# First block: output products from three f32r parts, a half of the columns at a time; the modulation computed inside the input projections

## The reference

```python
# first block, layer i
x = layer_norm(ALPHA * x + mixed @ w_out[i], ln_g[i, 0], ln_b[i, 0])
x = layer_norm(ALPHA * x + moe(x, ...), ln_g[i, 1], ln_b[i, 1])
# second block, layer l: the modulation depends on c and on weights only
shift, scale, gate = jnp.split(silu(c) @ ada_w[l] + ada_b[l], 3, axis=-1)
h = rms_norm(x, norm_w[l]) * (1.0 + scale) + shift
...
x = x + gate * (mixed @ w_out[l])
```

## Time and profile before

| | |
|---|---|
| median of 3 runs | 4140.01 us (4139.27 to 4143.25) |
| the profiled execution | 4143.35 us, span of its instructions 4141.7 us |
| mean granted clock of TensorE | 0.899 of 2.4 GHz |
| busy: TensorE / weight loads / VectorE / ACT / GpSimd | 3488.4 / 2668.9 / 1987.1 / 1367.8 / 445.2 us |
| read from HBM, written | 379.68 MB, 73.32 MB |

### The profile page before, as it was taken

How to read it: one execution, slowest core, us unless ns; L and a number is a source line. 1 busy time by engine, 2 the same in 40 slices (tenths; PEclk the granted TensorE clock), 3 DMA queues, 4 the chain that set the end, 5 groups by cost and what they waited for, 6 DMA issues and landing times. The chain is left out here.

```text
span 4141.7 us, 50920 instructions
## 1 busy us (share of the span) xinstructions
PE 3488.4 (84%) x19695; PEld 2668.9 (64%) x19695; DVE 1987.1 (48%) x3438; ACT 1367.8 (33%) x2478; POOL 445.2 (11%) x321
## 2 busy tenths in 40 slices
PE   8999886899829988847959999079988888998878
PEld 6874543788717766634438888068865576885557
DVE  3236455667461436462645756543245434315544
ACT  2026601657430023232025645220144322014442
POOL 0100000334330000000112423300010000001000
PEclk9999998999959899868979999589979998997999
DMA  4243062879540110015246966411100021110011
GB/s 146 89 126 108 1 228 93 299 264 395 196 176 26 50 29 1 1 31 148 102 144 247 346 231 261 182 67 32 31 1 1 31 92 63 32 31 1 1 49 79
DMA packets 247781, 458.80 MB, mean 111 GB/s; under 512 B 44754, under 2 KB 119846, under 8 KB 247206
## 3 DMA queue, kind: packets, MB, share of 16 engines
q1 hardware_dynamic: 229125, 388.64, 27.1%
q0 software_dynamic: 18432, 67.12, 4.2%
HBM read 379.68 MB, written 73.32 MB: 109 GB/s over the span
## 5 line engine op out<-in xcount | busy, mean ns | idle before, releaser
L1602 PE MATMUL psum<-high_in,e_rowsT_high 128*128 128x256 f32 (+1 forms) x1080 | 330.1, 324 | 5.4 <-DVE e_rowsT_low L174 5.4
L1603 PE MATMUL psum<-high_in,e_rowsT_low 128*128 128x256 f32 (+1 forms) x1080 | 326.2, 320 | 0.0
L174 POOL TENSOR_TENSOR low_down<-w_down,high_out 128x1024 fp32r<-128x1024 f32 x64 | 199.4, 3133 | 318.6 <-ACT high_out L1676 318.6
L1602 PEld LDWEIGHTS psum<-high_in,e_rowsT_high 128*128 128x128 f32 x1080 | 206.4, 191 | 22.3 <-issue 6.1
L1603 PEld LDWEIGHTS psum<-high_in,e_rowsT_low 128*128 128x128 f32 x1080 | 206.9, 192 | 16.2
L1183 POOL TENSOR_TENSOR x<-x,ln_bias 128x1024 f32<-128x1024 f32 x16 | 37.9, 2368 | 1313.1 <-DVE x L1157 1313.1
L3248 DVE TENSOR_REDUCE mla_low<-psum 128x1 f32<-128x256 f32 (+7 forms) x128 | 91.0, 752 | 153.2 <-PE psum L3114 153.2
L245 PE MATMUL psum<-ring_high,s_x_high 128*128 128x512 f32 (+3 forms) x768 | 140.1, 326 | 29.0 <-DVE ring_high L169 29.0
L174 DVE TENSOR_TENSOR low_gate<-w_gate,high_in 128x1024 fp32r<-128x1024 f32 x128 | 147.9, 1217 | 0.5 <-issue 0.5
L174 DVE TENSOR_TENSOR low_up<-w_up,high_in 128x1024 fp32r<-128x1024 f32 x128 | 147.9, 1217 | 0.0
L245 PEld LDWEIGHTS psum<-ring_high,s_x_high 128*128 128x128 f32 x768 | 117.2, 196 | 40.9 <-DVE ring_high L169 29.3
(11 more groups left out here) (570 smaller groups left out, 7905.4 us busy)
## 6 DMA issues: line engine op xcount, KB each, us to landing
w_gate<-in_exp_w_gate SPq DMA_DIRECT2D x32, 2048.0 KB, 10.1
w_up<-in_exp_w_up SPq DMA_DIRECT2D x32, 2048.0 KB, 15.1
w_down<-in_exp_w_down SPq DMA_DIRECT2D x32, 2048.0 KB, 21.4
ada<-in_ada_w SPq DMA_DIRECT2D x24, 1024.0 KB, 5.2
expert_rows<-e_out POOLq DMA_DIRECT2D x47, 512.0 KB, 7.0
expert_rows<-zero_row SPq DMA_DIRECT2D x33, 512.0 KB, 7.1
token_rows<-x SPq DMA_DIRECT2D x32, 512.0 KB, 2.6
x<-token_rows SPq DMA_DIRECT2D x24, 512.0 KB, 17.8
```

What stands on the lines that cost most here:

```text
L174: return eng.tensor_tensor(low, whole, high, ALU.subtract)
L1602: pe.matmul(dst, rows_high[:, k, :], w_high[:, k, cols], start=(k == 0), stop=False)
L1603: pe.matmul(dst, rows_low[:, k, :], w_high[:, k, cols], start=False, stop=False)
```

## The change

- **Output products of the first block.** Rows of the mixed features and weights are split into f32r high and low parts, and a product is made of three calls for each feature tile, as in the projections. The 1024 columns are done in halves: all eight row tiles for the first 512 columns, then all eight for the others. Eight banks instead of five. The statistics of a half are taken as soon as it is summed.
- **Early part.** In `memory_attention` SP loads the first half of the weights, and the mixer's 6 (layer 1: 8) feature tiles are split there, one an iteration, the high on ACT and the low on VectorE, each at the end of its iteration. The two memory tiles and the weights are split in `residual_norm`. In layer 1 the high parts of both weight halves share one place: ACT makes the second set after the eighth product (`shared_high`).
- **Order of loads** in `residual_norm`: x tile by tile, each with a semaphore of its own, the second half of the weights, gain and bias.
- **Modulation** moves from `residual_norm` into `project`: layer 0's beside the bias table, layer 1's beside the convolution. VectorE weighs one chunk after each even job from job 2 on, TensorE adds up a chunk after the even job that follows, SP loads two chunks for every chunk of projection weights, and waits for free slots there. ACT's Silu is its first instruction of the stage. The projection has five banks while the modulation is in it. Outputs from job 26 on wait until all chunks are weighed, since they lie where the slots do.
- **The gate row** is stored to DRAM at the end of the projection, and `gated_residual` loads it onto all partitions, behind the 4 MB of x.

Core of the diff:

```diff
+    banks = 5 if modulation else BANKS
     with stage(nc, "weights_loaded0", "weights_loaded1", "products_ready", "even_emptied", "odd_emptied",
-               "x_high", "x_low", "w_high", "w_low", *(beside.SEMAPHORES if beside else ())) as (block, s):
+               "x_high", "x_low", "w_high", "w_low", *(beside.SEMAPHORES if beside else ()),
+               *(modulation.SEMAPHORES if modulation else ())) as (block, s):
...
+                if modulation:
+                    modulation.load(sp, s, c)
                 if beside:
                     beside.store(sp, s, emptied, c)
...
                mm.then_inc(s["products_ready"], 1)
+                if modulation:
+                    modulation.add_up(pe, s, n)
...
+                    if modulation:
+                        modulation.before(eng, s, n)
+                    out(eng, core.bank[n % banks][0:shape[0], 0:shape[1]]).then_inc(emptied[parity], 1)
+                    if modulation and parity == 0:
+                        modulation.weigh(eng, s, n)
...
+            if modulation:
+                modulation.activate(act, s)
...
+        @block.sync
+        def _(sp):
+            for dst, view in weights.loads[0]:
+                sp.dma_start(dst, view).then_inc(s["out_weights"], 16)
+            sp.wait_ge(s["out_weights"], 16 * len(weights.loads[0]))
...
+                if 1 <= i <= len(early.whole):
+                    dve.wait_ge(s["early_high"], i)
+                    leave_low(dve, early.low[i - 1], early.whole[i - 1], early.high[i - 1]).then_inc(s["early_low"], 1)
...
+                if i < len(early.whole):
+                    act.activation(early.high[i], early.whole[i], ACT.Copy).then_inc(s["early_high"], 1)
...
+    mix = Halves(tiles_of(mixT), tiles_of(m.at("mix_low", AT_XT, [P, KT, SEQ], F32R)), tiles_of(m.at("mix_high", AT_WORK, [P, KT, SEQ], F32R)))
+    early = Halves(mix.whole[0:PAIRS], mix.low[0:PAIRS], mix.high[0:PAIRS])
+    loads, raws, lows, highs = [], [], [], []
+    for half in range(2):
+        raw = m.at("w_out", AT_WORK + (32 + 16 * half) * KB, [P, KT, BANK])
+        loads.append([(raw[:, :, :], rows_of(core.io["w_out"][0])[:, :, half * BANK:(half + 1) * BANK])])
+        raws.append(tiles_of(raw))
+        lows.append(tiles_of(m.at("w_out_low", AT_WORK + (32 + 16 * half) * KB, [P, KT, BANK], F32R)))
+        highs.append(tiles_of(m.at("w_out_high", AT_WORK + (64 + 16 * half) * KB, [P, KT, BANK], F32R)))
+    weights = OutWeights(loads, raws, lows, highs, False)
+    memory_attention(nc, core, qm, mixT[:, PAIRS:KT, :], AT_WORK + 96 * KB, weights, early)
+    return mix, weights
...
+    def load(self, sp, s, c):
         io, l = self.core.io, self.l
+        if c == 0:
+            with sp.bass.allow_non_contiguous_dma(reason="a few values a partition"):
+                sp.dma_start(self.c_col[:, :], io["c_2"][0].rearrange("(k p) -> p k", p=P)).then_inc(s["ada_loaded"], 16)
+                sp.dma_start(self.b_col[:, :], io["ada_b_2"][l, 0:2 * D].rearrange("(k p) -> p k", p=P)).then_inc(s["ada_loaded"], 16)
+                sp.dma_start(self.w_col[:, :], io["norm_w_2"][l].rearrange("(k p) -> p k", p=P)).then_inc(s["ada_loaded"], 16)
+            sp.dma_start(self.gate[:, :], broadcast_rows(io["ada_b_2"][l, 2 * D:3 * D])).then_inc(s["ada_loaded"], 16)
+        for j in range(self.SLOTS) if c == 1 else range(2 * c - 1, 2 * c + 1) if c >= 2 else ():
+            if j < self.CHUNKS:
+                if j >= self.SLOTS:
+                    sp.wait_ge(s["ada_ready"], j - self.SLOTS + 1)
+                view = rows_of(io["ada_w_2"][l])[:, :, j * self.WIDTH:(j + 1) * self.WIDTH]
+                sp.dma_start(self.slots[j % self.SLOTS][:, :, :], view).then_inc(s[f"ada_chunk{j % self.SLOTS}"], 16)
+
+    def store(self, sp, s):
+        sp.wait_ge(s["gate_ready"], 1)
+        sp.dma_start(self.core.mod_gates[self.l:self.l + 1, :], self.gate[0:1, :]).then_inc(s["gate_stored"], 16)
+        sp.wait_ge(s["gate_stored"], 16)
...
+    def before(self, eng, s, n):
+        if n >= 2 * self.CHUNKS + self.LAG:
+            eng.wait_ge(s["ada_ready"], self.CHUNKS)
+
+    def weigh(self, dve, s, n):
+
+
+
+        c = n // 2 - self.LAG // 2
+        if c == self.CHUNKS + 1:
+            self.finish(dve, s)
+        if not 0 <= c < self.CHUNKS:
+            return
...
+    def add_up(self, pe, s, n):
+        c = n // 2 - self.LAG // 2 - 1
+        if n % 2 or not 0 <= c < self.CHUNKS:
+            return
...
+    K = len(mix.whole)
+    OWN = K - 2
+    JOBS = 2 * TILES
...
+            for t in range(TILES):
+                sp.dma_start(x[:, t, :], source[t * P:(t + 1) * P, :]).then_inc(s[f"x_loaded{t}"], 16)
+            for dst, view in weights.loads[1]:
                 sp.dma_start(dst, view).then_inc(s["weights_loaded"], 16)
...
+            for n in range(JOBS):
+                half, t = divmod(n, TILES)
+                q = slice(t * P, (t + 1) * P)
+                dst = core.bank[n % BANKS][:, :]
+                high, low = weights.highs[half], weights.lows[half]
+                if n >= BANKS:
+                    pe.wait_ge(s["summed"], n - BANKS + 1)
+                for k in range(K):
+                    if t == 0:
+                        pe.wait_ge(s["w_high"], half * K + k + 1)
+                    if n == 0 and k >= OWN:
+                        pe.wait_ge(s["mem_high"], k - OWN + 1)
+                    pe.matmul(dst, mix.high[k][:, q], high[k], start=(k == 0), stop=False)
+                for k in range(K):
+                    if t == 0:
+                        pe.wait_ge(s["w_low"], half * K + k + 1)
+                    if n == 0 and k >= OWN:
+                        pe.wait_ge(s["mem_low"], k - OWN + 1)
+                    pe.matmul(dst, mix.high[k][:, q], low[k], start=False, stop=False)
+                    mm = pe.matmul(dst, mix.low[k][:, q], high[k], start=False, stop=(k == K - 1))
+            pe.wait_ge(s["summed"], JOBS)
...
+            def lows(half):
+                if half:
+                    dve.wait_ge(s["weights_loaded"], 16 * len(weights.loads[1]))
+                for k in range(K):
+                    if half == 0 and k >= OWN:
+                        dve.wait_ge(s["mem_high"], k - OWN + 1)
+                        leave_low(dve, mix.low[k], mix.whole[k], mix.high[k]).then_inc(s["mem_low"], 1)
+                    dve.wait_ge(s["w_high"], half * K + k + 1)
+                    leave_low(dve, weights.lows[half][k], weights.raws[half][k], weights.highs[half][k]).then_inc(s["w_low"], 1)
+            def add(t, half):
+                cols = slice(half * BANK, (half + 1) * BANK)
+                n = half * TILES + t
+                dve.wait_ge(s["products_ready"], n + 1)
+                if half == 0:
+                    dve.wait_ge(s[f"x_loaded{t}"], 16)
+                summed.settle(dve.scalar_tensor_tensor(out=x[:, t, cols], in0=x[:, t, cols], scalar=ALPHA, in1=core.bank[n % BANKS][:, :],
+                                                       op0=ALU.mult, op1=ALU.add))
+                measured.mark(dve.bn_stats(stats[:, t, half, :], x[:, t, cols]))
+            lows(0)
+            early = TILES if weights.shared_high else 2
+            for t in range(TILES):
+                add(t, 0)
+                if t == early - 1:
+                    lows(1)
+                    add(i, 1)
...
+            for half in range(2):
+                if half:
+                    act.wait_ge(s["weights_loaded"], 16 * len(weights.loads[1]))
+                    if weights.shared_high:
+                        act.wait_ge(s["products_ready"], TILES)
+                for k in range(K):
+                    if half == 0 and k >= OWN:
+                        act.activation(mix.high[k], mix.whole[k], ACT.Copy).then_inc(s["mem_high"], 1)
+                    act.activation(weights.highs[half][k], weights.raws[half][k], ACT.Copy).then_inc(s["w_high"], 1)
...
+    weights = OutWeights(loads, raws, lows, highs, True)
+    memory_attention(nc, core, qm, memT, W + 20 * KB, weights, early)
...
+            sp.dma_start(gate[:, :], broadcast_rows(gate_row)).then_inc(s["gate_loaded"], 16)
...
+            dve.wait_ge(s["gate_loaded"], 16)
```

176 lines of the change are left out of this document (67 added, 109 removed).

## The result

The changed kernel takes **4084.24 us** (median of 4 runs, 4082.28 to 4092.48) beside 4141.63 for the kernel before on the same chip (4139.27 to 4143.82): a ratio of 0.9865, 95% interval 0.9848 to 0.9882. So 57 us are gone where I had forecast 63.

What follows compares the result with a forecast made beforehand. TensorE alone was taken to bound the first block's output products, with weight loads ahead and a tail behind. Terms -36.5 - 44.0 - 8.6 + 14.4 + 3.5 + 5.5 + 2.5 = -63.2 us gave 4077 us, range 4064 to 4102.

Steps and rivals of the forecast that it cites:

- Part 1: Layer 0's output stage to the last sum: f32r calls and early weights take 93.8 us instead of 130.3, -36.5 us.
- Part 2: Layer 1's output stage to the last sum: 120.9 us instead of 164.9, -44.0 us.
- half-turn: Layer 1's products, eighth sum to ninth, where ACT makes the second set of highs: 10.5 us instead of 6.9.
- Part 3: Tails behind the last sum of both output stages: -4.3 us each, -8.6 together, bounds -4 and -12.
- Part 4: Modulation moved into the projections: add-ups +14.4 us for two layers; in layer 1 Silu +3.5, last chunk +5.5.
- last chunk: Layer 1's projection: the modulation's final load stands behind ring load 6, so TensorE waits, +5.5 us (3 to 12).
- Part 5: Memory attention with early highs and lows in each iteration: +2.5 us (0 to 10); gate row read back: nothing.
- (a): Output stage, second half: VectorE's normalisation becomes the bound, 1.5 us more 7 times in layer 0, 4087 us; chance 0.08.
- (b): Layer 1's projection takes its two late transfers at their far ends, 13 and 12 us, 4093 us; chance 0.08.
- (c): Projections: SP's new waits delay some 14 ring loads by three jobs (16.3 us), 4186 us; chance 0.03.
- (d): Output products: the parts don't pay at 1.2 GHz; a third of them so gives 4139 us, no change; chance 0.02.
- (e): Everything overlaps better: warm starts, tails at -12, memory attention for nothing, 4060 us; chance 0.03.

Runs made afterwards that it cites:

- all_mends: Changed kernel with Silu behind the highs, last chunk loaded earlier, layer 1's early parts begun later, four second-half highs in places of their own; 4064.74 us, ratio 0.9809.
- delay_long: Changed kernel with TensorE waiting, before layer 1's first memory attention scores, for two VectorE subtractions of 512 columns, some 1.3 us; 4084.49 us.
- parts_later: Changed kernel with layer 1's early parts begun in ACT's fourth round of the memory attention instead of the first; 4088.85 us.
- no_chunks: Changed kernel without the modulation's twelve chunks in both layers: none loaded, weighed or added up; 4057.84 us.

## Why the prediction was right, and where it was not

- **Layer 0's products (Part 1): right.** -35.8 against -36.5; first product at 12.9 (12 forecast), 5.44 us a job. Its clock was indeed low at the start, 0.60.
- **Layer 1's products (Part 2): right in its mechanism, mis-sized by 4.2 us.** The half-turn was given 10.5 us and took 13.34, because I priced ACT's ten highs and left out that TensorE, which stops for each of them, falls to the low clock behind them (0.75 over the job). In all_mends both are gone. The first product came at 15.2 instead of 13.6, also at the low clock (0.56). The bounds (14 and 18) held both.
- **Tails (Part 3): right**, -3.6 and -4.6 for -4.3 twice.
- **Modulation (Part 4): right in kind at each place**, add-ups 5.9 and 6.9 us for 7.2, Silu 6.0 for 3.5, last chunk 7.9 for 5.5. The transfers behind the last two were sized well: the gate row came 12.8 us after the stage's start (13.2 forecast), the last chunk landed 7.8 us after the ring load was issued (1358.44 to 1366.24; 7.4 forecast), and TensorE waited 5.86 us (5.5). What was left out is the low clock behind the wait, which stood only in the far bound: 0.58 over the first job, and 3.61 us instead of 2.01 for the eight calls behind the last chunk. The remark that the moved work leaves much GpSimd work for little holds in layer 1 only, where GpSimd is idle in the projection; in layer 0's it was busy 21.1 us, in the old output stage 19.0. No term hung on it. The gate row read back costs nothing: the first sum of the second block's output stage comes 28.6 us after the first load, before it was 28.2.
- **Memory attention (Part 5): wrong in layer 1.** The step priced ACT's and VectorE's extra work, which costs 0.2 us in layer 0 and 0.3 in layer 1 (44.9 us with all parts, 44.6 without). What it missed is that the stage takes 45 or 57 us (49 and 52.5 once each) by where TensorE's clock falls and rises, with the early parts or without them. The kernel before had the short one, and I took its 46 us for the stage's own. Layer 0's +0.2 is luck in part: its attention took 43.5 to 49.4 us in the traces of these kernels, 44.0 and 47.9 in the two of the changed kernel.
- **Unchanged code: assumed at zero, worth some -11 us** in this pair of traces. That the clock does it is argued from lengths and clocks, no run isolates it: the stretch from layer 1's transposes to the second block's first output stage took 1219.3 us at clock 0.89 before, 1209.5 at 0.90 in the changed kernel, and 1218.6 at 0.89 in delay_long, which has the changed kernel's code there. The forecast held because these and the last point are of opposite sign, not because I knew them: that part of the hit is luck.
- **Rivals.** (a) refuted by VectorE's 1.02 us of waiting in each round. (b) came a third of the way: 13.9 us for the two places, where the forecast had 9 and the rival 25. (c) nothing of it: layer 0's projection grew by its add-ups alone. (d) refuted: clock 1.00 in all f32r jobs of the output stages but the first product and the half-turn. (e) no: the starts ran at 0.60 and 0.56.

## What to carry to other kernels

Price an edit that fills a gap by what the gap does to TensorE's clock behind it: the last chunk's wait of 5.86 us cost 7.9, and the half-turn 6.4 us more than a job at full clock where 3.6 were counted. Where a stage is a chain of short bursts, compare its length over several executions and several builds before a change is blamed or credited; here the early parts went with the 11 us in six traces out of six, and parts_later and no_chunks refuted them. And look for a counterexample in kernels made for another purpose: no_chunks was one.

## What the runs showed of the hardware

- TensorE may stay at 1.2 GHz through a stretch in which it is busy without a pause: 14.00 of 14.00 us at clock 0.50 in the changed kernel's memory attention (1860.5 to 1874.5), against a rise after 9 to 15 us of bursts and pauses in seven kernels.
- Half a microsecond decides it: last fall 10.1 to 10.3 us before the first scores, rise 30.6 to 30.9 us after (seven traces); last fall 10.6 to 11.6 us before, rise 8.9 to 9.9 us after (five); last fall 9.9 or 8.7 us before, rise 14.0 or 15.2 us after. Why is open.
- The same build gave the same pattern again in layer 1's memory attention (57.2 us twice) and another one in layer 0's (44.0 and 47.9 us, clock 0.92 and 0.87). A stage's length in one trace can be one of several.
